# Recurrent gates computed per head of 64 channels, with the high and low parts of the operand stacked in 128 rows

## The reference: what is computed

```
r = sigmoid(einsum('bthi,hij->bthj', xh, wa) + ba)     # xh: xc by heads of 64
i = sigmoid(einsum('bthi,hij->bthj', xh, wx) + bx)
a = exp(-8 * r * softplus(-lam))
b = sqrt(1 - a*a) * (i * xc)
h[t] = a[t] * h[t-1] + b[t]
y_b = h * gelu(gate_lru)
```

## Time and profile before

| | |
|---|---|
| median of 3 runs | 1202.25 us (1200.2 to 1205.96) |
| the profiled execution | 1202.03 us, its span 1200.3 us |
| PE busy / weight loads busy | 1121.1 us (93%) / 995.4 us (83%) |
| DVE, ACT, POOL busy | 808.0 us (67%), 537.6 us (45%), 194.2 us (16%) |
| mean granted clock of TensorE | 0.977 |

### The profile page before, as it was taken

How to read it: one execution, slowest core, us unless ns; L and a number is a source line. 1 busy time by engine, 2 the same in 40 slices (tenths; PEclk the granted TensorE clock), 3 DMA queues, 4 the chain that set the end, 5 groups by cost and what they waited for, 6 DMA issues and landing times.

```text
span 1200.3 us, 20513 instructions
## 1 busy us (share of the span) xinstructions
PE 1121.1 (93%) x5736; PEld 995.4 (83%) x5737; DVE 808.0 (67%) x1532; ACT 537.6 (45%) x703; POOL 194.2 (16%) x189
## 2 busy tenths in 40 slices
PE   6999999999999999999999988899998999999970
PEld 6999999999999999978888867687887887777760
DVE  4666544374446456767777758797755898888884
ACT  4465343363336346422223312655544666656530
POOL 1000000010001000102222223406101132322322
PEclk9999999999999999999999999899999999999995
DMA  5331599747973742544444225896866789888563
GB/s 182 132 107 50 143 147 121 94 114 115 118 91 122 282 170 85 173 140 156 148 168 141 106 93 190 294 330 220 288 232 236 276 320 354 294 297 292 197 225 140
DMA packets 87274, 221.58 MB, mean 185 GB/s; under 512 B 19152, under 2 KB 45808, under 8 KB 80944
## 3 DMA queue, kind: packets, MB, share of 16 engines
q1 hardware_dynamic: 57824, 129.90, 33.1%
q0 software_dynamic: 18160, 59.53, 14.8%
q10 hardware_dynamic: 11232, 31.47, 13.7%
HBM read 133.75 MB, written 87.11 MB: 184 GB/s over the span
## 4 chain that ended last, share of the span: by engine, by line
PE 53%; DMA 16%; DVE 13%; issue 7%; ACT 6%; ACTq 2%; DVEq 2%; SPq 0%; POOL 0%; POOLq 0%
DMA y_scr<-yb 11%; PE ps_h L1484 9%; PE ps_vb_c L903 8%; PE ps_va_b L292 7%; PE ps_vb_c L292 7%; PE ps_va_b L903 6%; PE ps_o L1462 6%; PE ps_g L292 3%; PE ps_x L1451 2%; DMA gate<-g_scr 2%; DVE w_lo L1117 1%; PE ps_r_i L916 1%; ACT x_hi L1112 1%; PE ps_h L1513 1%; DVE yb L562 1%
## 5 line engine op out<-in xcount | busy, mean ns | idle before, releaser
L1484 PE MATMUL ps_h<-x_hi,xt_hi 128*128 x312 | 125.5, 402 | 3.0 <-issue 2.4
L292 PE MATMUL ps_vb_c<-x_hi,w_hi 128*128 (+1 forms) x320 | 114.6, 358 | 9.7 <-DVE x_lo L467 9.6
L1484 PE MATMUL ps_h<-x_hi,xt_lo 128*128 x312 | 122.0, 391 | 0.0
L1484 PE MATMUL ps_h<-w_lo,xt_hi 128*128 x312 | 121.7, 390 | 0.0
L292 PE MATMUL ps_vb_c<-x_hi,w_lo 128*128 (+1 forms) x320 | 113.9, 356 | 0.0
L292 PE MATMUL ps_vb_c<-x_lo,w_hi 128*128 (+1 forms) x320 | 113.3, 354 | 0.0
L292 PE MATMUL ps_va_b<-x_hi,w_lo 128*128 (+1 forms) x320 | 112.7, 352 | 0.0
L292 PE MATMUL ps_va_b<-x_hi,w_hi 128*128 (+1 forms) x320 | 112.6, 352 | 0.0
L292 PE MATMUL ps_va_b<-x_lo,w_hi 128*128 (+1 forms) x320 | 111.8, 349 | 0.0
L482 DVE SCALAR_TENSOR_TENSOR xc<-vb,par,xc 128x416 f32<-128x416 f32 (+1 forms) x60 | 39.1, 652 | 53.3 <-ACT xc L353 49.5
L1117 DVE TENSOR_TENSOR w_lo<-x_hi_p,x_hi 128x2048 f32 (+1 forms) x30 | 68.5, 2289 | 8.5 <-ACT x_hi L1112 6.8
(11 more groups left out here) (361 smaller groups left out, 2713.4 us busy)
## 6 DMA issues: line engine op xcount, KB each, us to landing
x_hi_p<-in_w SPq DMA_DIRECT2D x48, 1024.0 KB, 7.1
o_scr<-x_raw ACTq DMA_DIRECT2D x42, 512.0 KB, 7.7
w_lo_p<-xs_scr SPq DMA_DIRECT2D x41, 512.0 KB, 5.8
o_scr<-w_lo_p SPq DMA_DIRECT2D x41, 512.0 KB, 6.1
w_raw<-in_w_in POOLq DMA_DIRECT2D x19, 512.0 KB, 3.7
xs_scr<-x_raw ACTq DMA_DIRECT2D x18, 512.0 KB, 10.5
x_raw<-in_x_t SPq DMA_DIRECT2D x20, 416.0 KB, 3.4
x_hi_p<-y_scr SPq DMA_DIRECT2D x16, 512.0 KB, 4.2
```

Of the source, the lines that this page charges most:

```text
L292: mm = pe.matmul(ps[i][:, 0:CHUNK], w[:, i, k], x[:, k, bass.ds(c * CHUNK, CHUNK)], start=(k == 0 and n == 0), stop=(k == KT - 1 and n == 2))
L1484: mm = pe.matmul(ps_h[par][:], x[:, par, k], w[:, bass.ds(at, 1), k].rearrange("p o n -> p (o n)"), start=(k == 0 and n == 0), stop=(k == ...
```

## The change

The two heads of a group are handled apart. For each head the operand has 128 rows: 64 rows of the high part of its channels of `xc` and 64 rows of their low part (`xc_st[:, head]`). The head's weights stand twice, above each other, with the 64 columns of `r` beside the 64 of `i`. One matmul by `l_hi` then gives high by high plus high by low for both gates, and one by `l_lo` the rest: two matmuls per head, four in a round. (The product of the two low parts, left out before, is now in.) Head 0's bank holds `r` in rows 0 to 63 and `i` in 64 to 127, and head 1's the other way round. So the high part is two ACT instructions of 64 rows in place of one of 128, the low part two on DVE, and each gate's tanh two on ACT. The gate weights are loaded by six DMAs in place of one, with a semaphore of their own (`s_lraw`); the host's layout of `w_lru` stays.

```diff
-    xc_hi = sb("xc_hi", [P, LRU_N], F32R)
-    xc_lo = sb("xc_lo", [P, LRU_N], F32R)
+    xc_st = sb("xc_st", [P, 2, LRU_N], F32R)
...
+    def load_gates(pool, group):
+
+        gate = lambda rows, g, n: w_lru[group, rows, g:g + n, rows].rearrange("o p k n -> p (o k) n")
+        for rows in (low, high):
+            pool.dma_start(w_raw[rows, 1, 0].rearrange("p (k n) -> p k n", n=HALF), gate(low, 0, 2)).then_inc(s_lraw, 16)
+            for g in range(2):
+                pool.dma_start(w_raw[rows, 1, 1:2, (1 - g) * HALF:(2 - g) * HALF], gate(high, g, 1)).then_inc(s_lraw, 16)
...
-                    pool.dma_start(w_raw[:, i % 2, 0:2],
-                                   w_lru[bass.ds(j, 1)].rearrange("o p k n -> p (o k) n")).then_inc(s_wraw[i % 2], 16)
+                    load_gates(pool, bass.ds(j, 1))
...
-            for g, bank in enumerate((ps_r, ps_i)):
-                for n, (w, x) in enumerate(((l_hi, xc_hi), (l_hi, xc_lo), (l_lo, xc_hi))):
-                    mm = pe.matmul(bank[:, 0:LRU_N], w[:, g], x[:], start=(n == 0), stop=(n == 2))
+            for head, bank in enumerate((ps_ri, ps_ir)):
+                for n, w in enumerate((l_hi, l_lo)):
+                    mm = pe.matmul(bank[:, 0:LRU_N], w[:, head], xc_st[:, head], start=(n == 0), stop=(n == 1))
...
-                act.wait_ge(s_wraw[i % 2], 16 * (j * (WP // 2) + (i // 2 + i % 2)))
+                act.wait_ge(s_lraw, 16 * 6 * (j + 1))
...
-            act.activation(xc_hi[:], xc[:], ACT.Copy).then_inc(s_xch, 1)
+            act.activation(xc_st[low, 0], xc[low], ACT.Copy)
+            act.activation(xc_st[high, 1], xc[high], ACT.Copy).then_inc(s_xch, 1)
...
-            act.activation(yb[:], ps_r[:, 0:LRU_N], ACT.Tanh, scale=0.5, bias=hrb[:, bass.ds(j, 1)]).then_inc(s_thr, 1)
+            act.activation(yb[low], ps_ri[low, 0:LRU_N], ACT.Tanh, scale=0.5, bias=hrb[low, bass.ds(j, 1)])
+            act.activation(yb[high], ps_ir[high, 0:LRU_N], ACT.Tanh, scale=0.5, bias=hrb[high, bass.ds(j, 1)]).then_inc(s_thr, 1)
             act.wait_ge(s_b, q)
-            act.activation(i_t[:], ps_i[:, 0:LRU_N], ACT.Tanh, scale=0.5, bias=hib[:, bass.ds(j, 1)]).then_inc(s_thi, 1)
+            act.activation(i_t[low], ps_ri[high, 0:LRU_N], ACT.Tanh, scale=0.5, bias=hib[high, bass.ds(j, 1)])
+            act.activation(i_t[high], ps_ir[low, 0:LRU_N], ACT.Tanh, scale=0.5, bias=hib[low, bass.ds(j, 1)]).then_inc(s_thi, 1)
...
-            dve.tensor_tensor(xc_lo[:], xc[:], xc_hi[:].bitcast(F32), ALU.subtract).then_inc(s_xcl, 1)
+            dve.tensor_tensor(xc_st[high, 0], xc[low], xc_st[low, 0].bitcast(F32), ALU.subtract)
+            dve.tensor_tensor(xc_st[low, 1], xc[high], xc_st[high, 1].bitcast(F32), ALU.subtract).then_inc(s_xcl, 1)
...
-            dve.tensor_scalar(hib[:], par[:, :, IBIAS], 0.5, None, ALU.mult).then_inc(s_sp, 1)
+            dve.tensor_scalar(hib[low], par[high, :, IBIAS], 0.5, None, ALU.mult)
+            dve.tensor_scalar(hib[high], par[low, :, IBIAS], 0.5, None, ALU.mult).then_inc(s_sp, 1)
```

More of the change, by code:

```diff
@@ L26 @@
 P = 128
+HALF = P // 2
 D = 1024
@@ L135, in mixer @@
     ps_g = ctx.enter_context(nc.psum_tensor("ps_g", [P, 512], F32))
-    ps_vb, ps_c, ps_va, ps_b, ps_r, ps_i = (t[:, i] for t in (ps_vb_c, ps_va_b, ps_r_i) for i in range(2))
+    ps_vb, ps_c, ps_va, ps_b, ps_ri, ps_ir = (t[:, i] for t in (ps_vb_c, ps_va_b, ps_r_i) for i in range(2))
+    low, high = slice(0, HALF), slice(HALF, P)
     ps = [ps_vb, ps_c, ps_va, ps_b, ps_g]
@@ L158, in mixer @@
     s_wraw = [sem(f"s_wraw{i}") for i in range(2)]
+    s_lraw = sem("s_lraw")
     s_xraw = [sem(f"s_xraw{i}") for i in range(2)]
@@ L205, in mix_gpsimd @@
                 pool.wait_ge(s_wlo, i - 1)
-            dst = w_raw[:, i % 2] if i < MT else w_raw[:, i % 2, 0:2]
-            src = w_in[i] if i < MT else w_lru[0]
-            pool.dma_start(dst, src).then_inc(s_wraw[i % 2], 16)
+            if i < MT:
+                pool.dma_start(w_raw[:, i % 2], w_in[i]).then_inc(s_wraw[i % 2], 16)
+            else:
+                load_gates(pool, slice(0, 1))
         with pool.Fori(1, GROUPS) as j:
@@ L320, in split_w @@
                 act.wait_ge(s_w0, 16)
+            elif i < MT:
+                act.wait_ge(s_wraw[i % 2], 16 * (j * (WP // 2 - i % 2) + (i // 2 + i % 2)))
             else:
-                act.wait_ge(s_wraw[i % 2], 16 * (j * (WP // 2) + (i // 2 + i % 2)))
+                act.wait_ge(s_lraw, 16 * 6 * (j + 1))
             act.wait_ge(s_mm[i] if i < MT else s_ri, j * NCH)
@@ L328, in split_w_out @@
             if k < KT:
-                act.wait_ge(s_wraw[k % 2], 16 * (W_OUT // 2 + (k // 2 + k % 2)))
+                act.wait_ge(s_wraw[k % 2], 16 * (GROUPS * (WP // 2 - k % 2) + (k // 2 + k % 2)))
                 act.wait_ge(s_mm[MT - 1], READ)
```

## The result

The change makes the kernel slower: 1226.44 us in the median (1224.56 to 1235.68) against 1201.4 us, a ratio of 1.0221, 95% interval [1.0175, 1.0267]. The forecast was 1213.5 us: the sign and the place are right, the size is a little under half of what came, and the time lies above the range.

The account below looks back on a forecast made before the run. ACT, DVE and DMA bound about 144 to 400 us. From 1202.03: start +1.8, rounds 2-3 -0.76, round 4 +1.0, rounds 6-14 +9.0, round 15 split +1.0, rounds 15-18 -1.5, round 19 +1.0; together +11.5, 1213.5 us, range 1205 to 1220.

Parts of the forecast that it names:

- The loop sets rounds 5 to 15, not PE: Mixer, about 144 to 400 us: store landing, ACT, DVE and next store set the time; PE follows with little to spare.
- I take 0.50 for each extra one, 1.0 for a pair: ACT's gate tanh: each extra 64-row instruction costs 0.50 us, a round's two extra ones 1.0 where on the chain.
- twelve places: Rounds 0, 4, 6 to 14 and 19: the extra tanh pair lies on the chain, 1.0 us each.
- a backlog: Round 5: its store waits for DMA fills begun behind round 4, so the tanh pair there counts nothing.
- The split of `xc`: Extra ACT copy and DVE subtraction, about 0.5 us each, on the chain only in round 15: +1.0 us.
- The start: Rounds 0 and 1: extra subtraction 0.5, tanh pair 1.0 and gate loads 0.3 delay round 2, +1.8 us.
- The loads, 0.3: Round 0: six gate-weight loads instead of one make ACT wait some 0.3 to 0.5 us, taken as 0.3.
- The dead heat: Start of round 2: chunk 2's last piece ends at 61.76, PE starts at 61.91, so ACT or DVE delays hold it up.
- PE's saving: Two fewer gate matmuls save 0.38 us a round, counted in rounds 2, 3 and 15 to 18: -2.3 us.
- PE is the bound: Rival, whole mixer: PE sets the pace, 19 rounds win 0.38 us each, -7.2, last tanh +1.0: 1195.8 us; chance 0.09.
- Landings that do not move: Rival, rounds 6 to 8 and 10 to 12: DMA work sets landings, tanh pair vanishes, -6.0: 1207.5 us; chance 0.13.
- A dearer change: Rival: loads at 0.90 each (+4.4), extra tanh at 0.60 (+2.4), or round 5's pair and split (+2.0); first two 1220.3; chance 0.16.

Follow-up runs that it names:

- after_six: The changed kernel with six gate matmuls a round again, the high-part product run twice per head, output the same: 1237.5 us, ratio 1.0222 to the kernel before.
- after_bt: The changed kernel with the round's last product stored from `b_t` and the landing wait moved from ACT to DVE: 1213.28 us, ratio 1.0002 to the kernel before.
- four_mm: The kernel before with the gates' product of weights' low part and signal's high part left out, four matmuls a round: 1206.63 us, ratio 0.9953.
- before_bt: The kernel before with the last product stored from `b_t` and the landing wait moved from ACT to DVE: 1202.66 us, ratio 0.9925.
- rows64: The kernel before with only each gate tanh split into two instructions of 64 rows: 1235.3 us, ratio 1.0196.
- whole_tanh: The changed kernel with each gate tanh one instruction of 128 rows again, so r and i are mixed up: 1213.54 us, ratio 1.0021 to the kernel before.
- one_load: The changed kernel with gate weights stacked in memory, so one DMA replaces six: 1240.77 us, ratio 1.0241 to the kernel before.
- after_again: The changed kernel once more, unaltered, for a second profile: 1237.38 us, ratio 1.0215 to the kernel before.

## Why the prediction was half right

**The loop sets rounds 5 to 15, not PE:** right for the change. Its chain goes through the landings of rounds 6, 7 and 9 to 12 and meets no gate matmul between rounds 3 and 15, after_six gives PE its matmuls back at no cost that shows, and after_bt takes the tanh out of the loop and so wins back some 15 of 26 us. In the kernel before, the two sides were closer than I said: there less work on PE (four_mm, 0.9953) gains as well as a shorter loop (before_bt, 0.9925).

**The step that failed: "I take 0.50 for each extra one, 1.0 for a pair".** It is the term that was mis-sized. The pair costs 1.5 us (2.51 against 1.01 from the first tanh to the exp), and with nothing else of the change it made the kernel some 24 us slower (rows64) where my sum had 12 for it. I took the distance of two tanh that start at the same rows and applied it to four whose rows alternate. The upper bound, 0.60, was the busy time of one; but the overlap of the two tanh that were there already is lost as well, so the bound of a pair was not 1.2 but 1.5. The rule of the Trainium skill that I set beside it (page "ScalarE: Activation LUTs", section "What ACT_TABLE_LOAD costs") says rightly that half the rows are not half the time. The same section of the Trainium skill says that back-to-back ACTIVATEs overlap by about 93 ns; here they did so only at equal starting rows (by 0.09 to 0.14 us, otherwise not at all).

**Where the pair counts.** I had twelve places: rounds 0, 4, 6 to 14 and 19. The chain of the change has the fourth tanh in fourteen, with rounds 5 and 18 besides. Round 5, from that chain:

```profile
172.32 0.61 ACT i_t L394
...
176.50 3.36 ACTq L434
...
183.65 0.53 ACT vb L359
```

I counted nothing there, because that store would wait for a backlog. In the change it did not: it was issued at 179.21 us, landed 8.0 us later instead of 18.7, and ACT did not wait for it. The chain goes another way: the tanh delay ACT's own stream, the issues of the fills behind them (one of 3.36 us) and so the next round's `vb`. Fourteen times 1.5 is 21 us where I had 12. By this count, 9 of the 12.9 us by which the forecast lies under the median are the pair's. The 24 us of rows64 hold more than these 21: its projections took 4.0 us longer as well.

**The split of `xc`,** "+1.0 in round 15 only". On DVE:

```profile
188.76 0.59 DVE L503 TENSOR_TENSOR xc_st<-xc,xc_st 64x420 fp32r<-64x420 f32 x1 [1.19 <-ACT xc_st L375]
189.36 0.59 DVE L504 TENSOR_TENSOR xc_st<-xc,xc_st 64x420 fp32r<-64x420 f32 x1
189.98 0.59 DVE L510 TENSOR_TENSOR u<-ps_va_b,ya 128x416 f32<-128x416 f32 x1
```

The halves lie 0.60 apart against 0.51. The Trainium skill (page "VectorE: DVE Perf Modes", section "Two Vector instructions with no wait between them") has a rule for this: a DVE instruction that starts in another quadrant (group of 32 rows) than the one before, in what it reads or writes, is held until that one has ended. By the Trainium skill's rule the second half is held, and these rows agree. With ACT's second copy, 0.57, the split costs 1.2 us, and the chain of the change has the second subtraction in eight rounds, not in one: where the tanh had made ACT late, as in round 6, no wait for the store was left to cover it. With the tanh whole again (whole_tanh), matmuls, split and loads together cost 2.5 us, -0.4 to 5.4 by its interval.

**The start,** +1.8, came out at +3.7 (round 2 starts at 65.62 instead of 61.91). The chain there:

```profile
49.10 0.61 ACT i_t L394
...
59.15 0.56 ACT xc_st L375
...
60.34 0.59 DVE xc_st L504
...
65.62 0.50 PE ps_vb_c L303
```

The tanh of round 0 and both halves of round 1's split lie on it. The loads, 0.3, are not: one_load. The dead heat was seen rightly. What I did not price is what PE's wait does next: round 2 then takes 24.50 us instead of 22.93.

**PE's saving,** -2.3 us: the four matmuls are 0.77 us as foreseen, but none of it shows in the time: two more matmuls in each round cost nothing measurable (after_six).

**The rivals.** *PE is the bound*: refuted in the change; in the kernel before four_mm leaves it some room. *Landings that do not move*: refuted, the landings follow their issues with 17.5 to 18.3 us. *A dearer change* had the right sign but put most of its price on the loads, which cost nothing.

## What to carry to other kernels

Before work is cut into instructions of fewer rows, look where they start: on ScalarE and VectorE a half by rows cost a whole here, and it also took the overlap from its neighbours where the starting rows alternated; a half by columns cost 0.32 us of 0.51. A PE that looks 98% busy can run beside a loop of nearly its own length: ask the chain, and price what is added to that loop as well as what is taken from PE. And where a store's landing stands ahead of a string of instructions, let the store leave from a tile that is overwritten later in the round, so that the wait can stand behind them: that gave 0.75% here (0.48 to 1.02%).

## What was not expected of the hardware

- ACT instructions that start at other rows than the one before do not overlap with it, be it the rows read or those written: 0.62 us apart against 0.51 at equal rows, with the same busy time of 0.6 us.
- A long wait of PE was mostly paid twice: the projections of the next round, 22.84 us otherwise, ran partly at 1.2 GHz. In the change rounds 2, 6 and 16, behind waits of 3.6, 4.4 and 5.5 us, took 24.50, 23.67 and 24.68 us, and rounds 9, 11 and 12, behind 2.0, 2.0 and 2.5 us, took 24.29, 24.41 and 24.24, without one matmul more. But round 14 took only 22.86 behind 3.4 us, and in rows64 rounds 9 and 12 took 22.8 behind 2.9. Behind before's waits of up to 1.5 us the rounds took 22.8. So the length of the wait alone does not tell, and what I expected of after_again, a lower clock behind every wait of 2 us or more, held only for most of them.
